# Second feature pass of a two-block layer: seven products per quadrant scheme, in two token halves

## The reference

```python
return x + mixed @ w_out                                  # first layer
...
xn = _rms_norm(x, norm_g[l]) * (1.0 + sc_x) + sh_x        # second layer
fx_in, fx_gate, qx, kx, vx, nx_gate = _split_proj(xn @ w_in[l])
qx = _rms_norm(_heads(qx), q_norm_g[l])
kx = _rms_norm(_heads(kx), k_norm_g[l])
```

## Time and profile before

| | us |
|---|---|
| median of 3 runs | 3404.44 |
| lowest, highest | 3399.38, 3405.26 |
| the profiled execution | 3402.36 |
| its span in the trace | 3400.6 |

### The profile page before, as it was taken

One profiled execution on the slowest core, in us unless ns is written; L12 is line 12 of the kernel. 1 busy time (PEld: TensorE's weight loads), 2 busy tenths in 40 slices (PEclk: granted clock), 3 DMA queues, 4 the chain that ended last, 5 costly groups with the idle time before them and its releaser, 6 DMA issues. The chain is left out here.

```text
span 3400.6 us, 39668 instructions
## 1 busy us (share of the span) xinstructions
PE 3111.9 (92%) x14503; PEld 2445.2 (72%) x14503; DVE 1514.0 (45%) x2504; ACT 941.8 (28%) x1520; POOL 795.5 (23%) x842
## 2 busy tenths in 40 slices
PE   3799999999988999775998999899999898999899
PEld 2588887888876666553897877677888675666687
DVE  6643333042306666386455222476000145777633
ACT  4422212110112334342222234322011133555400
POOL 5322222111112222265342222011111041000111
PEclk7899999999998999778898999999999998999999
DMA  7534335122243341314102666323211235776475
GB/s 272 184 97 116 102 101 180 61 77 75 75 127 87 90 105 55 90 47 97 43 26 82 200 185 208 109 112 123 74 74 74 99 102 134 155 158 142 112 199 148
DMA packets 325559, 390.82 MB, mean 115 GB/s; under 512 B 93879, under 2 KB 260264, under 8 KB 310696
## 3 DMA queue, kind: packets, MB, share of 16 engines
q1 hardware_dynamic: 320692, 387.11, 39.9%
q10 hardware_dynamic: 4704, 1.59, 0.2%
HBM read 256.77 MB, written 135.79 MB: 115 GB/s over the span
## 5 line engine op out<-in xcount | busy, mean ns | idle before, releaser
L691 PE MATMUL f_psum_out<-f_x_high,f_w_high 128*128 128x512 f32 (+1 forms) x1472 | 573.5, 390 | 18.8 <-DVE f_x_low L668 8.1
L691 PE MATMUL f_psum_out<-f_x_low,f_w_high 128*128 128x512 f32 (+1 forms) x1472 | 569.0, 387 | 0.0
L691 PE MATMUL f_psum_out<-f_x_high,f_w_low 128*128 128x512 f32 (+1 forms) x1472 | 568.6, 386 | 0.0
L691 PEld LDWEIGHTS f_psum_out<-f_x_high,f_w_high 128*128 128x128 f32 x1472 | 279.1, 190 | 77.9 <-issue 15.0
L691 PEld LDWEIGHTS f_psum_out<-f_x_low,f_w_high 128*128 128x128 f32 x1472 | 278.9, 189 | 56.5 <-issue 1.7
L691 PEld LDWEIGHTS f_psum_out<-f_x_high,f_w_low 128*128 128x128 f32 x1472 | 278.9, 189 | 55.5
L1351 PE MATMUL nbr_psum_o<-nbr_probT,nbr_v 128*128 128x512 f32 (+3 forms) x576 | 235.8, 490 | 0.0
L683 POOL CAST f_w_high<-f_w 128x1024 fp32r<-128x1024 f32 x41 | 42.6, 1040 | 747.8 <-PE f_psum_out L691 550.5
L532 PE MATMUL p_psum_proj<-p_w_high,p_h_high 128*128 128x512 f32 x512 | 207.5, 405 | 7.4 <-issue 4.0
L532 PE MATMUL p_psum_proj<-p_w_low,p_h_high 128*128 128x512 f32 x512 | 202.1, 395 | 0.0
L532 PE MATMUL p_psum_proj<-p_w_high,p_h_low 128*128 128x512 f32 x512 | 202.1, 395 | 0.0
(11 more groups left out here) (541 smaller groups left out, 6134.0 us busy)
## 6 DMA issues: line engine op xcount, KB each, us to landing
f_w<-in_w_fm SPq DMA_DIRECT2D x45, 512.0 KB, 5.7
side_ada_w<-in_w_ada_rows SPq DMA_DIRECT2D x24, 512.0 KB, 5.7
scratch_qkmT<-p_qkT_out SPq DMA_DIRECT2D x32, 384.0 KB, 4.6
scratch_z1T<-f_out SPq DMA_DIRECT2D x10, 1024.0 KB, 4.8
p_z<-scratch_z1T SPq DMA_DIRECT2D x16, 640.0 KB, 6.6
p_xt<-in_x SPq DMA_DIRECT2D x16, 512.0 KB, 3.9
p_staging<-in_w_tok SPq DMA_DIRECT2D x8, 1024.0 KB, 8.0
scratch_hT<-p_h_slot SPq DMA_DIRECT2D x16, 512.0 KB, 3.3
```

Of the source, the lines that this page charges most:

```text
L691: last = nc.tensor.matmul(self.p_out[b][:, n * BANK + lo:n * BANK + hi], self.w_parts[b][w_part][:, k, :], self.x_parts[x_part][:, n, k, l ...
```

## The change

**The algebra.** With tokens split in even and odd tiles, x is a 2 x 2 matrix of quadrants B (K half by token tile parity); with a pair of feature blocks, the weights are a 2 x 2 matrix A. The product of two such matrices takes seven products of quadrants instead of eight, with four sums of A quadrants (`add_weights`, on GpSimd), four sums of B quadrants (`combine`, on GpSimd in the token tiles, for the last pair on VectorE) and seven additions of results, which are merges on VectorE, out of PSUM. `QuadrantPass` takes the place of `FeaturePass` here.

**The work list.** Tokens are taken in two halves of 1024, and an item is a pair of feature blocks in one half: 24 items of 7 products of 4 x 3 matmuls. A product fills one bank; six banks go round, and two hold the sums and transposes. In each half the order is `F2_ORDER`: a pair of queries or keys (0 to 3), then one of values (4, 5) or Fourier inputs (6, 7), then one of gates (8 to 11). All of this is written out, without loops.

**The norms.** TensorE gives two rows of sums per block; they are stored, read back over 128 partitions as 16 columns, rooted and inverted there, stored, and read back broadcast over the 64 partitions of each head. VectorE applies them after the last merge of the following item. Each output row then goes out, and the item after that writes into the same row.

**The token tiles** now store four quadrants and four combined ones in `x2q`. `begin_next` stands before tile 14 on all engines and `go_on` before tile 15. The input of the pass is seven pieces x0 to x6 of 128 x 2048 (1 MB) for each half.

```diff
+class QuadrantPass:
...
+    PRODUCTS = ((A11, B11), (S2, T2), (A12, B21), (S3, T3), (A22, T4), (S1, T1), (S4, B22))
+    N, HK, BANKS = 7, KB // 2, 6
...
+    def load_x(self, sp, half, i):
+        if half:
+            sp.wait_ge(self.prod_ready, self.N * (half * self.per_half - 1) + i + 1)
+        at = self.PRODUCTS[i][1] * self.HK
+        sp.dma_start(self.x[i][0][:], self.x_dram[:, at:at + self.HK, half * BANK:(half + 1) * BANK]).then_inc(self.x_in[i], 16)
...
+        nc.gpsimd.tensor_tensor(s1, a21, a22, ALU.add)
+        nc.gpsimd.tensor_tensor(s3, a11, a21, ALU.subtract)
+        pool.drain()
+        nc.gpsimd.tensor_tensor(s2, s1, a11, ALU.subtract)
+        pool.drain()
+        nc.gpsimd.tensor_tensor(s4, a12, s2, ALU.subtract).then_inc(self.sums_ready, 1)
...
+    def round_w(self, act, n, i):
+        a = self.PRODUCTS[i][0]
+        if n:
+            act.wait_ge(self.prod_ready, self.N * (n - 1) + i + 1)
+        if a < self.S1:
+            act.wait_ge(self.w_in[n % 2], 16 * (n // 2 + 1))
+        else:
+            act.wait_ge(self.sums_ready, n + 1)
...
+    def rest_of_w(self, pool, n, i):
+        pool.wait_ge(self.a_rounded, self.N * n + i + 1)
+        self.nc.gpsimd.tensor_tensor(self.a_low[:, i], self.quadrant(n, self.PRODUCTS[i][0]), self.a_high[:, i], ALU.subtract)\
+            .then_inc(self.a_ready, 1)
...
+    def product(self, pe, n, i):
+        pe.wait_ge(self.a_ready, self.N * n + i + 1)
+        if n % self.per_half == 0:
+            pe.wait_ge(self.x_ready[i], n // self.per_half + 1)
+        if self.N * n + i >= self.BANKS:
+            pe.wait_ge(self.prod_free, self.N * n + i + 1 - self.BANKS)
...
+        for k in range(self.HK):
+            for at, (w_part, x_part) in enumerate(PASSES):
+                last = self.nc.tensor.matmul(self.bank(n, i), a_parts[w_part][:, i, k, :], x_parts[x_part][:, k, :],
+                                             start=(k == 0 and at == 0), stop=(k == self.HK - 1 and at == len(PASSES) - 1))
+        last.then_inc(self.prod_ready, 1)
...
+        eng.wait_ge(combined_stored, 16 * (j + 1))
+        ops.tensor_tensor(t1, b12, b11, ALU.subtract)
+        ops.tensor_tensor(t3, b22, b12, ALU.subtract)
...
+        ops.tensor_tensor(t2, b22, t1, ALU.subtract)
...
+        ops.tensor_tensor(t4, t2, b21, ALU.subtract)
...
+                if b == 0:
+                    sp.dma_start(d["x2q"][:, 0:KB, of_pair], slot[0][:]).then_inc(slot_stored[0], 16)
+                else:
+                    sp.dma_start(d["x2q"][:, KB:KB + HK, of_pair], slot[1][:, HK:]).then_inc(slot_stored[1], 16)
...
+            def move_combined(j):
+                wait_apart(sp, combined_ready, j + 1, taken)
+                sp.dma_start(d["x2q"][:, KB + HK:, bass.ds(j * P, P)], combined[:].rearrange("p s k c -> p (s k) c"))\
+                    .then_inc(combined_stored, 16)
...
+                if b == 1 and not second:
+                    move_combined(j - 1)
...
+            def begin_next():
...
+                fp.load_w(sp, 0)
+                fp.load_x(sp, 0, 0)
+            def go_on():
+                sp.wait_ge(mix_ready[1], PAIRS)
+                sp.wait_ge(o_ready, NT - 1)
+                fp.load_x(sp, 0, 1)
                 sp.wait_ge(slices_used, 1)
-                fp.load_input(sp, d["x2T"], 0, 2)
-                sp.wait_ge(x1_ready[1], PAIRS)
-                fp.load_input(sp, d["x2T"], 2, 3)
+                fp.load_x(sp, 0, 2)
+                fp.load_x(sp, 0, 3)
+                sp.wait_ge(slices_used, 2)
+                fp.load_x(sp, 0, 4)
+                fp.load_x(sp, 0, 5)
...
+            tiles(sp, tile, begin_next, go_on)
+            sp.wait_ge(o_ready, NT)
+            fp.load_x(sp, 0, 6)
+            fp.load_w(sp, 1)
             move(PAIRS - 1, 1)
...
+                    if last and b == 1 and k == TURN_AT:
+                        turn_x(NT - 2)
...
+            for i in range(fp.BANKS):
+                if i == 4:
+                    pe.wait_ge(x_filled, NT)
+                fp.product(pe, 0, i)
+                if i == 1:
+                    turn_x(NT - 1)
...
+                act.wait_ge(combined_stored, 16 * (j + 1))
...
+                fp.round_x(act, 0, 0)
+                for i in range(fp.N):
+                    fp.round_w(act, 0, i)
+            def go_on():
+                fp.round_x(act, 0, 1)
+                fill(PAIRS - 1, 0)
+                fp.round_x(act, 0, 2)
+                fp.round_x(act, 0, 3)
...
+                if b == 0 and not first:
+                    wait_apart(pool, x_filled, 2 * j, taken)
+                    combine(pool, nc.gpsimd, j - 1)
...
+                fp.add_weights(pool, 0)
+                for i in range(fp.N):
+                    fp.rest_of_w(pool, 0, i)
...
+            def begin_next():
+                fp.rest_of_x(dve, nc.vector, 0, 0)
+            def go_on():
+                fp.rest_of_x(dve, nc.vector, 0, 1)
+                fp.rest_of_x(dve, nc.vector, 0, 2)
+            tiles(dve, tile, begin_next, go_on)
...
+F2_ORDER = (0, 4, 8, 1, 5, 9, 2, 6, 10, 3, 7, 11)
...
+            def spread_sums(n):
+                at = 2 * among(n, "qk")
+                for b in (1, 0):
+                    sp.wait_ge(rows_ready[b], at // 2 + 1)
...
+                    sp.dma_start(spread[b][:], d["rms_in"][at + b].rearrange("h (q c) -> (h q) c", q=HD)).then_inc(spread_in[b], 16)
...
+                    sp.wait_ge(rms_ready[b], at // 2 + 1)
+                    sp.dma_start(d["rms_out"][at + b].rearrange("h (q c) -> (h q) c", q=HD), spread[b][:]).then_inc(rms_stored[b], 16)
...
+                    for h in range(2):
+                        sp.dma_start(work[b][h * HD:(h + 1) * HD, :], d["rms_out"][at + b, h].partition_broadcast(HD))                            .then_inc(rms_in[b], 16)
...
+                if n + 2 <= LAST:
+                    fp.load_w(sp, n + 2)
+                if kind(n - 1) == "qk":
+                    spread_sums(n - 1)
+                if kind(n - 1) in ("qk", "v"):
+                    store(n - 1)
+                if n == fp.per_half - 1:
+                    for i in range(N):
+                        fp.load_x(sp, 1, i)
+                if kind(n) in ("in", "gate"):
+                    store(n)
+            sp.wait_ge(high_stored, 32 * among(LAST + 1, "qk"))
...
+                    dve.wait_ge(rms_in[b], 32 * (among(n, "qk") + 1))
+                    nc.vector.scalar_tensor_tensor(x[:], x[:], gain[:, is_key:is_key + 1], work[b][:], ALU.mult, ALU.mult)
...
+                    if before:
+                        dve.wait_ge(high_stored, 16 * before)
+                    nc.vector.tensor_copy(high[:], x[:]).then_inc(high_ready, 1)
+                    dve.drain()
+                    nc.vector.tensor_tensor(x[:].bitcast(F32R), x[:], high[:], ALU.subtract).then_inc(low_ready[b], 1)
...
+                if n >= 2:
+                    dve.wait_ge(stored[n % 2][b], 16 * (n // 2))
...
+                if i == 0:
+                    await_row(n, 0)
+                    nc.vector.tensor_copy(column(first, 0), bank(n, 0)).then_inc(fp.prod_free, 1)
+                elif i == 1:
+                    dve.drain()
+                    nc.vector.tensor_tensor(whole(u2), column(first, 0), bank(n, 1), ALU.add).then_inc(fp.prod_free, 1)
...
+                elif i == 6:
+                    nc.vector.tensor_tensor(column(first, 1), whole(u2), bank(n, 6), ALU.add).then_inc(fp.prod_free, 1)
+                    dve.drain().then_inc(out_ready[0], 1)
```

More of the change, by code:

```diff
@@ L2175, in tile @@
                     turn_y(j + 1, b)
-                if not first:
+                if not first and not (last and b == 1):
                     turn_x(2 * j + b - 1, first=second)
@@ L2375, in turn_v @@
-            def turn_v(j, b):
-                pe.wait_ge(vT_ready[b], j - FIRST_V + 1)
-                for n in range(NT):
-                    last = nc.tensor.transpose(fp.p_out[b][:, n * P:(n + 1) * P], row[b][:, n * P:(n + 1) * P], g.ident[:])
-                last.then_inc(v_turned[b], 1)
-            def pairs(first, end, second):
-                with pe.Fori(first, end) as j:
-                    project(j, 1, lambda: second(j, 0))
-                    project(j + 1, 0, lambda: second(j, 1))
@@ L2397, in _ @@
+            pe.wait_ge(ones_ready, 1)
+            for n in range(LAST + 1):
+                for i in range(N):
+                    if n or i >= fp.BANKS:
+                        fp.product(pe, n, i)
+                    for b in range(2):
+                        if i == ASIDE[kind(n - 1)][b]:
+                            aside(n - 1, b)
         @block.gpsimd
```

439 lines of the change are left out of this document (275 added, 164 removed).

## The result

The changed kernel takes 3421.04 us (median of 5, 3415.85 to 3424.14), the kernel before 3400.25 us (3399.15 to 3405.26); the ratio is 1.0054 (95% interval 1.0042 to 1.0067). The forecast was 3370 us, with 3343 to 3397 as its range. The profiled execution after has a span of 3422.4 us, 21.8 us more than before.

A forecast was written before the change was run, and what follows sets the result against it. TensorE was taken to bound the second feature pass. Products -65.3, change-over +16, chain +13, half-way switch +3, token tiles 0 and end -1 sum to -34.3, giving 3370 us against the median; range 3343 to 3397, held at 0.8.

The forecast's parts named there:

- the chain: Behind queries and keys, roots to merge 0: 2.5 us late after four pairs, 0.7 after four others; +13 us.
- the half-way switch: Seven 1 MB loads of x following item 11's products: VectorE ends slightly late with collisions; +3 us, between 0 and +9.
- the small rows: Terms outside the main steps: token tiles 0, end of the pass -1 us.
- The products: In the second feature pass, 2016 matmuls in place of 2304, new boundaries costed at nothing; -65.3 us.
- The change-over: From token tiles to item 1's first product: 36.5 us lost against 20 before, with a collision; +16 us.
- second cause: At the change-over, ScalarE's copy of tile 14 waits for the combined store; TensorE idles 19 us before the last transposes.
- the 20 us lost before: In the old kernel's pass, some 20 us lost by about 2180, in waits and at a lower clock behind them.
- The first cause: At the change-over, VectorE takes x0's low part ahead of tile 14's addition, so tile 15 starts late; 10 us.
- rival (b): Chain behind queries and keys late by 6 us at each pair: 40 in place of 13, 3397 us; chance 0.09.
- The sign: Whole kernel: faster 0.83, same 0.07, slower 0.10; turning once the chain is some 6 us late on average.
- rival (c): Slower than before: merge 0 behind the norms, four hops at 5.7 us, chain costs 104, 3461 us; chance 0.10.

The follow-up runs named there:

- the copy on reading: Against the changed kernel, ScalarE's copy of tile 14 waits until GpSimd has read the slot, not until the combined quadrants are stored; 3405.67 us, ratio 1.0004.
- x0_later: Against the changed kernel, VectorE takes the low part of x0 behind the addition that empties tile 14, not ahead of it; 3419.72 us, ratio 1.0061.
- x_on_scalar: Against the changed kernel, ScalarE instead of SyncE issues the seven loads of x at the half-way switch; 3418.42 us, ratio 1.0049.

## Why the prediction was wrong, step by step

Forecast and measured sum are 56.1 us apart. 17.5 of these are waits of the chain, 9.9 waits at the half-way switch, 23.8 the lower clock behind waits, and 4.9 the small rows.

**The products** were right: 2016 matmuls, 2.72 us for a product where nothing waits; and the groups of 12 cost nothing, as taken from the earlier trace rows.

**The change-over** was right in its times (2108.75, 2147.25 and 2169.82 against 2108.7, 2148.5 and 2169.8) and in its second cause, the combined store, which the copy on reading shows at 9.6 of the 10 us expected of it. The close match of the clock times has some luck in it: the addition of tile 13 came 1.0 us later than before. TensorE's idle time before the last transposes was 15.8 us where 19 were forecast, since tile 15 began at the lower clock and took longer; VectorE sets the time of the transposes, so this cost nothing. The trace before also has waits of 2.03, 2.31 and 2.19 us (at 2119.32, 2132.89 and 2182.73) that the forecast doesn't list; its 20 us lost were a difference of times and hold them. The first cause, x0 ahead of the addition, is a wait but not a cost: x0_later gives nothing back, since GpSimd has the weights of item 0 ahead of the inverse of tile 14. "10 us" as a cost of this order was the wrong reading of two waits in a row.

**The chain** is the step that failed, in the term "six operations of the chain are of that kind: +2 us". The mechanism was found and its size was not: three kinds of operation collide, casts among them, and the six take 11.1 us where they take 6.4 to 6.5 without GpSimd, +4.7 in place of +2. The row for the collision, 2.73 us against 0.68, was one operation, and its surplus of 2 us was taken once for all six. Six times that would have been too much: five of the operations took 0.9 to 1.0 us longer, and the first multiplication none. The last store adds 0.6 where values went before. So the chain is 3.0 to 6.0 us late at seven pairs, not 2.5 and 0.7 at eight. The 1.8 us more of TensorE's work behind values is there as forecast, but slower stores behind values, slower hops in items 5 and 20 and the idle GpSimd in item 11 hide it. Its waits, 30.5 us, lie between the 13 of the forecast and the 40 of rival (b), which had been given 0.09.

**The lower clock** was left out altogether, though the section on the bound names it among the 20 us lost before. Behind the waits for merge 0 stand 16.1 us of slower matmuls, behind item 1's start 3.3, at the switch 4.4: 23.8 us that no term of the sum held. Without them the changed kernel would come out at about 21.8 - 23.8 = -2 us, so the late chain and the switch took the gain away, and the clock gave the sign. With a clock loss in the same proportion rival (b) itself is slower than before, by an estimate. "The sign turns once it is some 6 us late on average" was wrong for the same reason: without the chain 46.6 - 21.8 = 24.8 us of gain would be left, and at 46.6 / 30.5 us for each us of wait, an estimate, they are used up when eight waits are 2.0 us each. Measured were 3.8.

**The half-way switch** was costed at the rate of the loads alone, from the product that frees each piece. SyncE reaches them at 2421.7, some 16 us later, behind the norm stores of item 9, and 3 MB of stores and weights issued from 2417.5 on go ahead. The step failed by leaving out what is queued in front of the moved transfers: 12.9 us of waits in place of 3. x_on_scalar shows that going past that queue costs as much.

**The sign** was given to the slower side at 0.10, for one mechanism, the chain (rival (c)). The place was right, merge 0 behind the norms. The reason was not: (c) had four transfers at 5.7 us each, and the first two took 5.9 to 7.2 us together, about as forecast, and the stores 2.6 to 3.7. The chain cost less than half the price that (c) named (46.6 against 104), and it took the switch and the clock as well to make the kernel slower.

## What to carry to other kernels

When a tuned stage is bound by one engine without waits, price each new wait twice: the wait, and the slow stretch of TensorE behind it, which here was about half as long again. For a chain that must end within a fixed time, apply the collision to every operation that can have it, and look first at what in the chain can simply begin earlier: here the roots, whose input had been there for 5 to 9 us, were worth 1.4% of the whole (1.0054 to 0.9918). Where waits stand in a row on one engine, price the removal of one by what the engine will wait for next: undoing the second gave 9.6 us here, undoing the first nothing.

## What was not expected of the hardware

The clock of TensorE fell behind waits of about 2 us (granted 0.72 over the 6 us behind 2.17 and 2.59 us) and did not behind others of 2.16 and 2.95 (1.00 and 0.98). The size of the wait from 2 to 6 us changed the slow time little, where the clock fell: 1.9 to 3.6 us.

Beside loads of 1 MB from another engine's queue, a store of 512 KB took 8.3 us in place of 2.6, and the last of its chain 5.9 in place of 2.7, so a store on a critical chain is not safe from a transfer merely because that one stands in another queue.
